# A down projection with twelve instead of ten Strassen pairs, and some of its sums on VectorE instead of POOL

## What is computed

```python
h = rms_norm(x, ln_mix_w)
proj = h @ w_in                       # 2048 x 9216
y_a = multiscale_pool(u_pool) @ w_branch_a
y_b = hgrn2(q, f_logit, inp, g) @ w_branch_b      # a recurrence over chunks of 64 positions
x = x + (sigmoid(gate_a) * y_a + sigmoid(gate_b) * y_b) @ w_out
u = causal_depthwise_conv(rms_norm(x, ln_ffn_w) @ w_up)
x = x + (silu(u_gate) * u_val) @ w_down           # 5504 x 2048: the down projection
x = x + sigmoid(rms_norm(x, ln_ple_w) @ w_ple_gate) * (p @ w_ple)
return rms_norm(x, ln_final_w)
```

## Time and profile before

| | us |
|---|---|
| median of three runs | 1438.48 (1438.47 to 4224.24) |
| profiled execution | 1438.39 |
| its span, from the first to the last instruction | 1436.6 |
| PE busy | 1425.5 |
| DVE busy | 985.1 |
| ACT busy | 760.0 |
| POOL busy | 216.9 |

### The profile page before, as it was taken

One profiled execution on the slowest core, in us unless ns is written; L12 is line 12 of the kernel. 1 busy time (PEld: TensorE's weight loads), 2 busy tenths in 40 slices (PEclk: granted clock), 3 DMA queues, 4 the chain that ended last, 5 costly groups with the idle time before them and its releaser, 6 DMA issues.

```text
span 1436.6 us, 19705 instructions
## 1 busy us (share of the span) xinstructions
PE 1425.5 (99%) x7112; PEld 1212.1 (84%) x7112; DVE 985.1 (69%) x1180; ACT 760.0 (53%) x920; POOL 216.9 (15%) x153
## 2 busy tenths in 40 slices
PE   9999999999999999999999999999999999999997
PEld 7888888888888888888888888888888888888886
DVE  7576777845455455566777777777777887787755
ACT  7555655544444444555555555555555546554544
POOL 0044144100000000000101101111011531140000
PEclk9999999999999999999999999999999999999999
DMA  9765555456666655465666566565665656565653
GB/s 325 225 205 161 165 176 159 143 194 190 191 190 191 191 190 188 158 208 181 190 188 191 180 198 186 179 204 175 191 193 177 212 192 200 177 213 188 227 200 121
DMA packets 190875, 273.47 MB, mean 190 GB/s; under 512 B 11744, under 2 KB 103136, under 8 KB 190688
## 3 DMA queue, kind: packets, MB, share of 16 engines
q1 hardware_dynamic: 190384, 272.30, 59.6%
q10 hardware_dynamic: 432, 0.37, 0.1%
HBM read 270.53 MB, written 2.10 MB: 190 GB/s over the span
## 4 chain that ended last, share of the span: by engine, by line
PE 98%; DVE 1%; issue 1%; ACT 0%; ACTq 0%; POOLq 0%; POOL 0%; DVEq 0%
PE main L622 15%; PE main L624 15%; PE main L623 15%; PE aux L747 11%; PE main L747 11%; PE aux L756 6%; PE main L756 6%; PE main L672 3%; PE main L670 3%; PE main L671 3%; PE aux L670 3%; PE aux L672 3%; PE aux L671 3%; PE aux L788 1%; PE aux L818 1%
## 5 line engine op out<-in xcount | busy, mean ns | idle before, releaser
L1301 DVE TENSOR_TENSOR w_lo<-raw,w_hi 128x1024 fp32r<-128x1024 f32 (+1 forms) x490 | 612.4, 1260 | 394.5 <-ACT w_hi L1009 394.3
L1009 ACT ACTIVATE w_hi<-raw 128x1024 fp32r<-128x1024 f32 (+1 forms) x490 | 514.1, 1052 | 541.2 <-PE main L624 284.8
L622 PE MATMUL main<-w_hi,xT 128*128 128x512 f32 x702 | 276.8, 394 | 0.0
L624 PE MATMUL main<-w_hi,xT 128*128 128x512 f32 x702 | 273.6, 390 | 0.0
L623 PE MATMUL main<-w_lo,xT 128*128 128x512 f32 x702 | 273.6, 390 | 0.0
L747 PE MATMUL aux<-xT,w_hi 128*128 128x512 f32 x704 | 169.9, 391 | 0.0
L747 PE MATMUL main<-xT,w_hi 128*128 128x512 f32 x672 | 163.0, 391 | 0.0
L624 PEld LDWEIGHTS main<-w_hi,xT 128*128 128x128 f32 x702 | 131.9, 188 | 27.4
L622 PEld LDWEIGHTS main<-w_hi,xT 128*128 128x128 f32 x702 | 132.0, 188 | 27.0 <-issue 0.4
L623 PEld LDWEIGHTS main<-w_lo,xT 128*128 128x128 f32 x702 | 132.0, 188 | 26.1
L747 PEld LDWEIGHTS aux<-xT,w_hi 128*128 128x128 f32 x704 | 129.4, 188 | 25.2 <-issue 0.3
(11 more groups left out here) (270 smaller groups left out, 1770.7 us busy)
## 6 DMA issues: line engine op xcount, KB each, us to landing
raw<-in_w_up SPq DMA_DIRECT2D x336, 256.0 KB
raw<-in_w_in SPq DMA_DIRECT2D x136, 512.0 KB
raw<-in_w_down SPq DMA_DIRECT2D x84, 512.0 KB
raw<-in_w_out SPq DMA_DIRECT2D x32, 512.0 KB
raw<-in_w_ple_gate SPq DMA_DIRECT2D x32, 512.0 KB
raw<-in_w_branch_a SPq DMA_DIRECT2D x16, 512.0 KB
raw<-in_w_branch_b SPq DMA_DIRECT2D x16, 512.0 KB
raw<-in_w_in SPq DMA_DIRECT2D x15, 256.0 KB, 5.7
```

The source lines that it names most:

```text
L622: pe.matmul(acc, th, wh, start=first, stop=False)
L624: return pe.matmul(acc, tl, wh, start=False, stop=end)
L1009: ac.activation(w_hi[:, u % RING, :, 0:w], raw[:, u % RING, :, 0:w], ACT.Copy).then_inc(hi_full, 1)
L1301: dve.tensor_tensor(w_lo[:, u % RING, :, 0:w], raw[:, u % RING, :, 0:w], w_hi[:, u % RING, :, 0:w].bitcast(F32), ALU.subtract).then_inc(lo ...
```

## The change

The pairs of either half become six, at i = 5, 7, 10, 12, 15, 17; two successive pairs are now alternately two and three row tile pairs apart. POOL's `act_sums` is cut down to its joining instruction (`join_act`), and VectorE's new `act_sums` does the four sums of 128 x 128 in the slot of the weight sums, behind them. `a_sums_hi` and `a_sums_lo` get two buffers, so that ScalarE waits for the products of the pair before the last instead of the last. The weight sums' first instruction has a semaphore of its own, `w_diffs`. The transposes of x and what follows them come one unit later, those of the recurrence's output for g = 1 two units later.

```diff
-OBT = [PV[g] + 4 for g in range(2)]
+OBT = [PV[g] + 4 + 2 * g for g in range(2)]
...
-SEVEN_AT = ((5, 8, 11, 14, 17), (5, 8, 11, 14, 17))
+SEVEN_AT = ((5, 7, 10, 12, 15, 17), (5, 7, 10, 12, 15, 17))
...
-X2_AT = {down_slot(n) + 1: n for n in range(NQ)}
+X2_AT = {down_slot(n) + 2: n for n in range(NQ)}
...
-        a_sums_hi = sb("a_sums_hi", [P, 4, P], F32R, ffn)
-        a_sums_lo = sb("a_sums_lo", [P, 4, P], F32R, ffn)
+        a_sums_hi = sb("a_sums_hi", [P, 2, 4, P], F32R, ffn)
+        a_sums_lo = sb("a_sums_lo", [P, 2, 4, P], F32R, ffn)
...
-                    if q:
-                        ac.wait_ge(w_sums_done, 2 * q)
+                    if q > 1:
+                        ac.wait_ge(w_sums_done, 2 * (q - 1))
...
-                    ac.wait_ge(w_summed, 3 * q + (1, 3)[half])
+                    ac.wait_ge(w_summed if half else w_diffs, 2 * (q + 1) if half else q + 1)
...
-                        if s == at + 2:
+                        if s == at + 1 + norm:
...
-            def weight_sums(u):
+            def weight_diffs(u):
...
+                if q:
+                    dve.wait_ge(w_sums_ready, 2 * q)
...
+            def act_sums(q):
+
+                dve.wait_ge(a_joined, q + 1)
+                a = a_sums[:].rearrange("p k (b t) -> p k b t", t=P)
+                a11, a12, a21, a22 = a[:, 0, 0], a[:, 1, 0], a[:, 0, 1], a[:, 1, 1]
+                dve.tensor_tensor(a22, a21, a22, ALU.add).then_inc(a_sum_part, 1)
+                dve.wait_ge(a_sum_part, 3 * q + 1)
+                dve.tensor_tensor(a21, a11, a21, ALU.subtract).then_inc(a_sum_part, 1)
+                dve.wait_ge(a_sum_part, 3 * q + 2)
+                dve.tensor_tensor(a11, a22, a11, ALU.subtract).then_inc(a_sum_part, 1)
+                dve.wait_ge(a_sum_part, 3 * q + 3)
+                dve.tensor_tensor(a12, a12, a11, ALU.subtract).then_inc(a_summed, 1)
...
                 if s + 2 in SEVEN:
-                    weight_sums(s + 2)
+                    weight_diffs(s + 2)
+                    act_sums(SEVEN[s + 2])
...
-            def act_sums(u, q):
+            def join_act(u, q):
...
                 pool.tensor_tensor(a_sums[:], aT_hi[:, k:k + 2, :].bitcast(F32), aT_lo[:, k:k + 2, :].bitcast(F32),
-                                   ALU.add).then_inc(a_sum_part, 1)
-                pool.wait_ge(a_sum_part, done + 1)
-                pool.tensor_tensor(a22, a21, a22, ALU.add).then_inc(a_sum_part, 1)
...
+                                   ALU.add).then_inc(a_joined, 1)
```

More of the change, by code:

```diff
@@ L355, in build @@
             sem, ("pT_hi_ready", "pT_ready", "sig_ready", "emb_ready", "y_pre"))
[L357 to L360, removed]
+        w_diffs, w_summed, w_sums_hi_ready, w_sums_ready, w_sums_done = map(
+            sem, ("w_diffs", "w_summed", "w_sums_hi_ready", "w_sums_ready", "w_sums_done"))
+        a_joined, a_sum_part, a_summed, a_sums_hi_ready, a_sums_ready = map(
+            sem, ("a_joined", "a_sum_part", "a_summed", "a_sums_hi_ready", "a_sums_ready"))
         x2_turned, copied, combined = map(sem, ("x2_turned", "copied", "combined"))
@@ L675, in act_block, with act_sum @@
                 return aT_hi[:, k, tb * P:(tb + 1) * P], aT_lo[:, k, tb * P:(tb + 1) * P]
-            def act_sum(k):
-                return a_sums_hi[:, k, :], a_sums_lo[:, k, :]
+            def act_sum(q, k):
+                return a_sums_hi[:, q % 2, k, :], a_sums_lo[:, q % 2, k, :]
             def ring_tile(u, t):
@@ L710, in down_seven @@
                     pe.wait_ge(a_sums_ready, q + 1)
-                    mm = triple(down_acc(2 * p + 1, 0), *act_sum(2), *ring_tile(u, 1), start=False, stop=False)
+                    mm = triple(down_acc(2 * p + 1, 0), *act_sum(q, 2), *ring_tile(u, 1), start=False, stop=False)
                 mm.then_inc(units_done, 1)
@@ L719, in down_sums @@
                 if half == 0:
-                    triple(product(p, 1), *act_sum(3), *sum_tile(0), start=first, stop=end)
-                    mm = triple(product(p, 3), *act_sum(1), *sum_tile(1), start=first, stop=end)
+                    triple(product(p, 1), *act_sum(q, 3), *sum_tile(0), start=first, stop=end)
+                    mm = triple(product(p, 3), *act_sum(q, 1), *sum_tile(1), start=first, stop=end)
                 else:
-                    triple(product(p, 2), *act_sum(0), *sum_tile(2), start=first, stop=end)
+                    triple(product(p, 2), *act_sum(q, 0), *sum_tile(2), start=first, stop=end)
                     mm = triple(down_acc(2 * p, 1), *act_block(2 * i + 1, 1), *sum_tile(3), start=False, stop=False)
@@ L1553, in sums_lo @@
                     dve.wait_ge(a_sums_hi_ready, q + 1)
-                    dve.tensor_tensor(a_sums_lo[:].rearrange("p k t -> p (k t)"), a_sums[:].rearrange("p k t -> p (k t)"),
-                                      a_sums_hi[:].rearrange("p k t -> p (k t)").bitcast(F32), ALU.subtract).then_inc(a_sums_ready, 1)
+                    dve.tensor_tensor(a_sums_lo[:, q % 2].rearrange("p k t -> p (k t)"), a_sums[:].rearrange("p k t -> p (k t)"),
+                                      a_sums_hi[:, q % 2].rearrange("p k t -> p (k t)").bitcast(F32), ALU.subtract).then_inc(a_sums_ready, 1)
                 else:
@@ L1846, in _ @@
             for q, u in enumerate(SEVENS):
-                act_sums(u, q)
+                join_act(u, q)
             root(2)
```

21 lines of the change are left out of this document (6 added, 15 removed).

## The result

The changed kernel takes 1444.07 us (median of 7 runs, 1443.81 to 1444.22) against 1438.48 for the kernel before: a ratio of 1.0039, with a 95% interval of 1.0026 to 1.0051. It is slower by 5.6 us, which counts as within 2%. The prediction, 1442.6 us in a range of 1435.8 to 1445.8, was 1.5 us under. The profiled span grew from 1436.6 to 1442.4 us, by 5.8. One of the seven runs of the kernel before took 4224.24 us, and the ratio leaves it out; the other six lie between 1438.38 and 1438.69.

What follows compares the result with a forecast made beforehand. TensorE, busy 1425.5 of 1436.6 us, was taken as the bound. Savings of 3.89 us from the median 1438.48 gave 1434.6; new stops of 8.04 made 1442.6 us, range 1435.8 to 1445.8.

Steps and rivals of the forecast that it cites:

- What goes: Savings on TensorE: six matmuls 1.36, recurrence output's transpose wait 0.78, two x transpose waits 1.46, old first-pair stop 0.29; 3.89 us.
- The fourth rival: Moved transposes only shift their wait to the gate units; 1445.3 us at most; chance 0.11 shared with dear sums.
- The sums: Each new 128-column sum on VectorE takes 0.285 us plus 0.04 for handing over; four add 1.16 us.
- The short gap: Between pairs two row tile pairs apart, VectorE needs 11.01 us while TensorE's 45 matmuls take 10.19.
- The first rival: VectorE keeps up and TensorE never stops for the sums: 1434.6 us; chance of under 1436, 0.09.
- the second: Rival: stops at the pairs are there but small, with 0.21 us a sum: 1438.9 us; chance 0.19.
- third: Rival: sums as dear as 256 columns, 0.46 us each: 1447.1 us; chance 0.11 shared with a shifted wait.
- It stops for 0.82: TensorE's stop at a pair ending a short gap, plus 0.11 for the step after: 0.93 us at i = 12 and 17.
- i = 5: First pair of a half, behind the up projection's tail on VectorE: TensorE loses 0.43 us, 0.05 of it handing over.
- i = 7: Pair after the first: ScalarE, waiting for the sums, starts the short gap 0.8 us late; 0.93 + 0.80 = 1.73 us.

Runs made afterwards that it cites:

- The run with one sum: The changed kernel without the first three of the four 128-column sums of every pair, so the products take other operands: 1436.32 us.
- The run with the sums first: The changed kernel with the four activation sums ahead of the weight sums instead of behind them: 1444.20 us.
- the last two kernels: Kernel before with moved transposes, eleven pairs three apart, combining in three units: second half alone, or both halves with first-half pairs one row tile pair later: 1435.50, 1435.49 us.
- the run with the sums one pair ahead: The changed kernel with two buffers for activation sums, the next pair's four sums made right behind this pair's `a_sums_lo`: 1445.07 us.
- the run with POOL's sums: The changed kernel, twelve pairs, with the four sums of 128 columns given back to POOL behind its joining sum: 1440.97 us.

## Why the prediction was right

**What goes.** Six matmuls: as said, 1.36 us. The stops at the transposes: both waits for x are gone, 1.47 (said: 1.46), and the one for the recurrence's output, 0.78, is gone whole, as said. Run alone, the moved transposes gave 2.5 us, a little more than the 2.24 of the two terms; the shorter groups of transposes make up about 0.15 of that. The fourth rival, a wait shifted to the gate, did not come.

**The sums.** Said: 0.285 us and 0.04 for handing over. The trace has 0.28 to 0.29 and steps of 0.32. "VectorE: DVE Perf Modes", section "The TRN2 errata", of the Trainium skill gave an estimate of 291 ns; the group of the second sums agrees (ns: least, median, most):

```profile
L1559 DVE TENSOR_TENSOR a_sums<-a_sums x12: 291/292/293, 1123.0 to 1308.9; 128x128 f32<-128x128 f32 x12
```

**The short gap.** Said: a chain of 11.01 us against 10.19. Measured: 11.07. The first rival, VectorE keeping up, falls by that row, and the second and third by the sums' own length.

**The step that was mis-sized** is "It stops for 0.82, and each stop costs about 0.11 more for the step after it". Measured at i = 12 it is 1.02 and 0.08. The chain's excess is 0.88, as said within 0.06; what is missing is the time from the end of `a_sums_lo` to TensorE's start, 0.15 us (1164.79 to 1164.94), of which the prediction counted 0.05 at i = 5 and nothing elsewhere.

**What was not foreseen**: at seven of the pairs TensorE meets the products of the weight sums just in time, and the first step there is about 0.10 us too long. Behind i = 7 the pass that TensorE needs ends at 1140.07 + 1.21 = 1141.28, and TensorE starts at 1141.34; at the seven the distance is 0.06 to 0.08, at the others 0.43 and more, and there the step is an ordinary one.

```profile
1140.07 1.21 DVE L1574 TENSOR_TENSOR xT<-w_sums,xT 128x1024 fp32r<-128x1024 f32 x1
```

And in the down projection 92 steps are too long by 0.002 to 0.014 us, together 0.56, against 16 steps and 0.09 before (from the starts before rounding). The account of the down projection:

| us | said | measured |
|---|---|---|
| stops at `a_sums_lo`, eight | 7.16 | 8.06 |
| steps behind them, eight (0.11 each, 0.08 each) | 0.88 | 0.64 |
| first steps in the weight sums' products, seven | 0 | 0.70 |
| small steps, more than before | 0 | 0.47 |
| together | 8.04 | 9.87 |

Less 1.36 for the matmuls, 1.47 and 0.78 for the transposes and 0.29 for the old first stop, 9.87 leaves 5.97, 0.2 more than the 5.8 by which the span grew; the shorter groups of transposes make up about 0.15 of that. So the prediction was short by 0.90 in the stops and by 1.17 in two lines that it did not have, and over by 0.24 in the steps behind the stops.

**i = 5 was right in size for a wrong reason.** The prediction put its stop down to the tail of the up projection. The second half, which has no such tail, stops for the same 0.47. The chain there starts with a half split that waits for ScalarE, and ScalarE for a buffer that TensorE gives back, so it starts the same 5.88 us ahead of the time at which TensorE, unstopped, would read the sums, in both halves. From 1119.52 to `a_sums_lo`'s end at 1125.04 + 0.68 it lasts 6.20 us (said: 6.15), and 6.20 + 0.15 - 5.88 is the stop of 0.47. So the size came out close by luck. The rows:

```profile
1119.52 0.69 DVE L1298 TENSOR_TENSOR w_lo<-raw,w_hi 128x512 fp32r<-128x512 f32 x1 [0.57 <-ACT w_hi L1007]
...
1125.04 0.68 DVE L1569 TENSOR_TENSOR a_sums_lo<-a_sums,a_sums_hi 128x512 fp32r<-128x512 f32 x1
1126.58 1.60 DVE L1301 TENSOR_TENSOR w_lo<-raw,w_hi 128x1024 fp32r<-128x1024 f32 x1 [0.86 <-ACT w_hi L1009]
```

The tail of the up projection may account for the stop of the kernel before, which its first half alone has and which went when the first pair was put two units later; the tail itself was not taken away in any run.

**i = 7.** Said: 0.8 us late by ScalarE, 1.73 in all. The last row shows it: VectorE starts the gap at 1126.58, 0.72 after TensorE's 1125.86, and TensorE's own longer steps give back about 0.2 of it: a stop of 1.53. The run with one sum leaves a stop at i = 7 alone; there the lateness is 0.20, a wait of 0.15 comes in the gap, and ScalarE's share cannot be told from that run alone. The run with the sums first took this wait away and put others in its place, so it doesn't measure it.

Left open is why the small steps are longer, and why the last two kernels keep about 0.3 us at one pair and lose 0.2 in the gate; neither was tried.

## What to carry to other kernels

Weigh an added step against the gap in which it must be done, not against an engine's mean share: VectorE was busy 69% of the span and yet 0.9 us short between two deadlines, and 0.96 us taken out of that gap gave back 0.98 at the stop. In the run that put the work in another order in the same gap, it was only late for another reader. Waits of 0.7 to 0.8 us at the transposes went when these were issued one or two units later: that edit alone gave 2.5 us, while the other two lost 8.1 together.

## What was not expected of the hardware

An instruction of VectorE that meets one of POOL on SBUF loses time by when it starts, not a fixed share. Behind the first pair the changed kernel's joining sum runs from 1125.79, as POOL's timeline has it:

```profile
1125.79 1.29 POOL L1839 TENSOR_TENSOR a_sums<-aT_hi,aT_lo 128x512 f32<-128x512 f32 x1 [7.92 <-DVE a_sums_lo L1569]
```

It cost the split that started 0.79 us into it, at 1126.58, 0.37 (1.60 instead of 1.23). In the run with the sums one pair ahead it cost a 0.29 us sum that started 0.15 into it 1.00. Where VectorE was busy without a break, both suffered: the joining sum took 2.20 us, and the pass behind it 2.32 instead of 1.21, as POOL's and VectorE's rows of the run with POOL's sums show:

```profile
1163.93 2.20 POOL L1838 TENSOR_TENSOR a_sums<-aT_hi,aT_lo 128x512 f32<-128x512 f32 x1 [4.95 <-DVE a_sums_lo L1569]
```

```profile
1163.77 1.22 DVE L1301 TENSOR_TENSOR w_lo<-raw,w_hi 128x1024 fp32r<-128x1024 f32 x1
1164.90 2.32 DVE L1574 TENSOR_TENSOR xT<-w_sums,xT 128x1024 fp32r<-128x1024 f32 x1
```

In these three the loss is the time from VectorE's start to the end of POOL's instruction, less 0.12 to 0.15 us: 1125.79 + 1.29 - 1126.58 = 0.50 against 0.37, 1153.82 + 1.30 - 1153.97 = 1.15 against 1.00, and 1163.93 + 2.20 - 1164.90 = 1.23 against 1.11. The small sum on POOL fits as well: 1153.44 + 1.33 - 1154.37 = 0.40, where the pass lost 0.27. "SBUF — State Buffer", section "Who interferes with whom", of the Trainium skill says that the later of two such instructions blocks until the other ends; the rows agree but for that 0.12 to 0.15. The prediction took 0.3 for each joining sum from one row. That held (0.35 to 0.38 in the changed kernel) because VectorE happened to be waiting when the joining sum started, as it is at the start of every short gap there.
